# Two stacks of hybrid layers on one core: operands, sums of squares, factors and a bias table at the borders between projections

## The chip, the core and the metric

The kernel runs on one core of a Trainium2 chip. The metric is the device time of one execution in microseconds; less is better. The engines are named as in the profile: PE (TensorE), DVE (VectorE), ACT (ScalarE), POOL (GpSimd) and SP (SyncE, which here only issues DMAs).

## The reference

Two stacks of two layers each work on one sequence of 1024 positions by 1024 channels in float32. Cut to what matters for the change:

```python
# stack 1 (called stack 0 in the kernel), for both layers
h = rmsnorm(x, norm_g); proj = h @ w_in          # 28 blocks of 128 columns
y = concat(conv module, gated conv, windowed attention, neighbourhood attention with bias table)
x = x + y @ w_out                                # after both layers: x = rmsnorm(x, final_norm_g)
# stack 2 (stack 1 in the kernel), for both layers
u = rmsnorm(h, attn_norm); proj = u @ w_in       # 24 blocks
h = h + concat(retention, differential attention with ALiBi) @ w_out
h = h + (silu(u2 @ w_gate) * (u2 @ w_up)) @ w_down,   u2 = rmsnorm(h, ffn_norm)
out = rmsnorm(h, final_norm)
```

A row factor of an rmsnorm is 1/sqrt(mean of squares over the 1024 channels). Between the stacks two such norms follow each other directly.

## The kernel before

The activations lie transposed: `xt` holds 8 chunks of 128 channels by 1024 positions. A float32 product is made of three products of rounded parts: each operand is split into a high part and the rest. For the activations ACT rounds a chunk into `in_hi` (`split_hi`, line 1098) and DVE subtracts it into `in_lo` (`split_lo`, lines 1540 with gains and 1543 without); for the weights POOL does both (`split`, lines 597 and 601), one block of 128 output columns at a time, into two slots. SP loads the raw blocks (`load`, line 511). `product` (line 696) makes one output block: for each chunk three operand pairs, each with two matmuls of 512 columns, 24 steps with 8 chunks and 12 with 4. `between` is a list of other PE work that is put at evenly spaced steps inside the product. A product signals `done`; DVE takes its result out of PSUM with `evacuate` (line 1525, times the row factor `rfac`) or `add_to_x` (line 1531) and signals `taken`. Product n waits until block n - 2 is taken.

The row factor: ACT squares a chunk of x (`squares`, line 1102; `squares_of_half` also squares without the gain, line 1117, for the norm between the stacks), DVE adds the eight squares into one accumulator (`sum_squares`, line 1549; `sum_squares_x`, line 1575), PE sums over partitions (`row_sums`, line 716), DVE takes the inverse root and writes it on the diagonals of tiles (`row_factor`, lines 1597 to 1614), PE spreads it over all partitions (`spread`, line 724), ACT copies it to `rfac` (`take_factor`, line 1128). Before the change the squares lie in SBUF slots SQ and SQ_X.

The order of work is written out by hand for every engine, and each engine works through its own list in order, with semaphores between them. In stack 0 a layer has blocks 0 to 27 (projections, with attention, convolution and norms between them), 28 to 35 (first half of the output projection, chunks 0 to 3 of the mixed values) and 36 to 43 (second half). In stack 1 the blocks are 0 to 23, 24 to 31, 32 to 39 and 40 to 63 (FFN down projection). The last products of the second half are followed by the first product of the next layer, whose operands come from the x that they finish: `add_half` on DVE and `squares_of_half` on ACT work on that border.

The bias table of the neighbourhood attention is loaded by three DMAs from ACT's queue (line 1316), in pieces of 256 bytes, into `space_lo`, which is the memory of chunks 4 to 7 of `in_lo`; so ACT waits for the end of block 27 first. ACT then rounds chunks 1 to 3 for block 28, and takes the transposed values (`take_values`, line 1133).

## Time and profile before

| | us |
|---|---|
| median of 3 runs | 3616.26 |
| lowest and highest | 3616.20, 3618.64 |
| profiled execution, its own time | 3617.75 |
| its span in the profile | 3615.9 |
| PE busy | 3429.6 |
| POOL busy | 1353.8 |
| DVE busy | 1990.3 |
| ACT busy | 994.2 |

The profile is of one execution. A page has the busy time of each engine, the span in 40 slices, the chain of work that ended last, and groups of instructions by line. The trace behind it can be asked for the waits of an engine with what ended each, and for a timeline. In a timeline row the first number is the start and the second the time until the end; "x8" says that eight instructions are merged, and [7.14 <-DVE in_lo L1543] that the engine stood idle for 7.14 us until DVE's instruction of line 1543 let it go on.

### The profile page before, as it was taken

The numbers are of one execution on the slowest core, as the hardware profiler recorded it, in microseconds if no ns is written. First come the engines' busy times: TensorE is split into PE (matmuls) and PEld (weight loads), VectorE is DVE, ScalarE is ACT, GpSimd is POOL, SyncE is SP. The second block draws the span as 40 slices with busy tenths as digits, with TensorE's granted clock in tenths as the row PEclk, the third lists the DMA queues.
The fourth block names the chain that finished last, engine by engine and source line by source line (L and its number), as shares of the span: only waits on it lengthen the run. The fifth ranks groups of instructions, "written<-read, shape, count | busy, mean of one in ns | idle before, by whom it ended". The sixth has DMA issues, their size and how long they took to land.

```text
span 3615.9 us, 41963 instructions
## 1 busy us (share of the span) xinstructions
PE 3429.6 (95%) x16504; PEld 2769.6 (77%) x16504; DVE 1990.3 (55%) x2939; ACT 994.2 (27%) x1863; POOL 1353.8 (37%) x593
## 2 busy tenths in 40 slices
PE   7999899999898999898999999999998989999997
PEld 6877677877776888666888888888875778888886
DVE  5668536668547324577656642351438675565326
ACT  2220342130243000364333330010016543333101
POOL 3324213424303432203655534543220156554343
PEclk9999999999998999999999999999999999999998
DMA  4111203101201111102222252111110032223322
GB/s 147 42 31 52 55 13 87 42 30 53 67 7 35 41 50 38 53 1 93 72 86 88 82 198 81 52 53 54 35 64 7 16 125 77 86 88 120 131 87 76
DMA packets 72524, 236.31 MB, mean 65 GB/s; under 512 B 21920, under 2 KB 22304, under 8 KB 66208
## 3 DMA queue, kind: packets, MB, share of 16 engines
q1 hardware_dynamic: 50112, 205.54, 17.0%
q10 hardware_dynamic: 22240, 28.38, 2.7%
q8 instruction: 119, 1.95, 0.2%
q14 instruction: 53, 0.43, 0.0%
HBM read 193.00 MB, written 37.75 MB: 64 GB/s over the span
## 4 chain that ended last, share of the span: by engine, by line
PE 59%; DVE 6%; issue 1%; ACT 1%; DVEq 0%; ACTq 0%
PE ps L696 30%; PE ps L1063 23%; PE ps L759 2%; PE ps L823 1%; DVE space_hi L1660 1%; DVE xt L1531 1%; PE ps L806 0%; DVE st L1549 0%; DVE sl_r L2124 0%; ACT st L1166 0%; PE ps L983 0%; PE ps L979 0%; PE ps L735 0%; PE ps L834 0%; DVE small L1589 0%
## 5 line engine op out<-in xcount | busy, mean ns | idle before, releaser
L597 POOL TENSOR_TENSOR w_hi<-w_raw,ones_r 128x1024 fp32r<-128x1024 f32 x184 | 362.5, 1970 | 1836.6 <-PE ps L696 1813.7
L1063 PE MATMUL ps<-sl_r,sl_r 128*128 128x512 f32 x3696 | 843.9, 391 | 22.9 <-issue 22.9
L1063 PEld LDWEIGHTS ps<-sl_r,sl_r 128*128 128x128 f32 x3696 | 696.9, 189 | 168.8 <-issue 23.7
L696 PE MATMUL ps<-in_hi,w_hi 128*128 128x512 f32 x2176 | 700.4, 403 | 50.3 <-DVE in_lo L1540 19.5
L696 PE MATMUL ps<-in_hi,w_lo 128*128 128x512 f32 x2176 | 683.1, 395 | 0.0
L696 PE MATMUL ps<-in_lo,w_hi 128*128 128x512 f32 x2176 | 681.5, 395 | 0.0
L601 POOL TENSOR_TENSOR w_lo<-w_raw,w_hi 128x1024 fp32r<-128x1024 f32 x184 | 512.4, 2785 | 14.4
L696 PEld LDWEIGHTS ps<-in_hi,w_hi 128*128 128x128 f32 x2176 | 397.3, 190 | 156.8 <-issue 55.7
L696 PEld LDWEIGHTS ps<-in_lo,w_hi 128*128 128x128 f32 x2176 | 410.4, 190 | 91.2 <-issue 4.4
L696 PEld LDWEIGHTS ps<-in_hi,w_lo 128*128 128x128 f32 x2176 | 408.1, 190 | 92.2 <-issue 5.8
L696 PE MATMUL ps<-sl_r,w_hi 128*128 128x512 f32 x1408 | 378.5, 391 | 4.7 <-DVE sl_r L2166 4.7
L1525 DVE TENSOR_TENSOR st<-ps,rfac 128x1024 f32<-128x1024 f32 x104 | 127.2, 1223 | 410.2 <-PE ps L696 393.4
L641 POOL TENSOR_TENSOR sl_r<-sl,sl_r 128x1024 fp32r<-128x1024 f32 x88 | 212.5, 2416 | 343.9 <-ACT sl_r L1416 343.9
L1531 DVE TENSOR_TENSOR xt<-xt,ps 128x1024 f32<-128x1024 f32 x112 | 136.7, 1220 | 363.3 <-PE ps L696 362.3
L2134 DVE TENSOR_TENSOR sl_r<-raw_pair,sl_r 128x1024 fp32r<-128x1024 f32 x88 | 206.0, 2378 | 218.3 <-ACT sl_r L1416 218.2
L696 PEld LDWEIGHTS ps<-sl_r,w_hi 128*128 128x128 f32 x1408 | 265.5, 189 | 60.9 <-DVE sl_r L2166 5.6
L1180 ACT ACTIVATE st<-ps 128x384 f32<-128x384 f32 (+3 forms) x256 | 122.7, 479 | 348.9 <-PE ps L806 348.6
L696 PE MATMUL ps<-sl_r,w_lo 128*128 128x512 f32 x704 | 218.2, 391 | 0.0
L823 PEld LDWEIGHTS ps<-st 128*128 128x128 f32 x1504 | 184.4, 193 | 34.1 <-ACT st L1180 15.3
L823 PE MATMUL ps<-st 128*128 128x64 f32 (+1 forms) x1504 | 199.1, 275 | 5.8 <-DVE st L1709 5.8
L1808 DVE SCALAR_TENSOR_TENSOR st<-st,cur 128x1023 f32<-128x1023 f32 (+14 forms) x128 | 191.9, 1499 | 1.8
L1427 ACT ACTIVATE ps<-ps 128x512 f32<-128x512 f32 x132 | 76.8, 582 | 301.6 <-PE ps L1063 301.6
(198 smaller groups left out, 3457.1 us busy)
## 6 DMA issues: line engine op xcount, KB each, us to landing
w_raw<-w_in SPq DMA_DIRECT2D x184, 512.0 KB, 3.6
raw_pair<-w_ffn SPq DMA_DIRECT2D x44, 1024.0 KB, 4.9
hid_kept<-sl SPq DMA_DIRECT2D x44, 512.0 KB, 2.6
sl<-hid_kept SPq DMA_DIRECT2D x44, 512.0 KB, 7.3
x_put_away<-xt SPq DMA_DIRECT2D x16, 512.0 KB, 7.8
xt<-x_put_away SPq DMA_DIRECT2D x16, 512.0 KB, 6.4
xt<-x_in ACTq DMA_DIRECT2D x8, 512.0 KB, 9.1
space_lo<-c_alibi ACTq DMA_DIRECT2D x2, 2048.0 KB, 7.9
```

The source lines that it names most:

```text
L597: pool.tensor_tensor(w_hi[:, j, :], w_raw[:, j, :], ones[:, 0:1].broadcast_to([P, KC * P]), ALU.mult).then_inc(pool_own, 1)
L601: pool.tensor_tensor(w_lo[:, j, :], w_raw[:, j, :], w_hi[:, j, :].bitcast(F32), ALU.subtract).then_inc(w_split.handle, 1)
L641: pool.tensor_tensor(sl_r[:, RING[p % 2][lo], :], pair_sums(p)[i], sl_r[:, RING[p % 2][hi], :].bitcast(F32), ALU.subtract).then_inc(pair_s ...
L696: last = pe.matmul(ps[:, 2 * j + h, :], w[:, w_slot, (w_k + k) * P:(w_k + k + 1) * P], part[:, k0 + k, h * HALF:(h + 1) * HALF], start=(k ...
L823: last = pe.matmul(ps[:, 7, t * width:(t + 1) * width], turned_buffer(kind, g)[:, b * P:(b + 1) * P], value(t, kt), start=(kt == tiles[0]) ...
L1063: last = pe.matmul(ps[:, to[name], :], ring(sl_r, p, wp[w])[:, k * P:(k + 1) * P], half_of(sl_r, xp[x], k), start=(name in ("P1", "P5") an ...
L1180: act.activation(turned_buffer(kind, g)[:, 0:w], ps[:, 6, 0:w], ACT.Copy).then_inc(turned_out.handle, 1)
L1427: act.activation(to, ps[:, of, :], ACT.Copy).then_inc(carried.handle, 1)
L1525: dve.tensor_tensor(to, ps[:, 2 * j:2 * j + 2, :].rearrange("p a b -> p (a b)"), rfac[:, :], ALU.mult).then_inc(taken.handle, 1)
L1531: last = dve.tensor_tensor(xt[:, c, :], xt[:, c, :], flat(ps, 2 * (n % 2), 2), ALU.add)
L1808: return dve.scalar_tensor_tensor(acc[:, a:b], source[:, a + d:b + d], weight, acc[:, a:b], ALU.mult, ALU.add)
L2134: dve.tensor_tensor(lo, source, hi.bitcast(F32), ALU.subtract).then_inc(pair_lo.handle, 1)
```

## The change

- The squares of all borders but those at the FFN's entry go to PSUM banks 4 to 7, and DVE adds them from there. At the start of the kernel all chunks are rounded and subtracted first, and squared and summed behind that.
- Start: the second weight load waits for x chunk 3; DVE instead of POOL makes the first block's `w_lo`; three small DMAs are issued later; the lambda arithmetic of stack 1 moves behind evacuation 2. In layer 0 of stack 0 the row sums stand inside product 1; in both layers its spread moves from step 18 to step 21.
- Blocks 27 (stack 0) and 23 (stack 1): the product signals when chunks 0 to 3 have been read for the last time, and ACT and DVE write the operands of the next half from then on, DVE ahead of the block's evacuation. The last transposition of values moves from in front of block 28 (24) into block 29 (25). In stack 1 the ALiBi load and DVE's wait for it come later.
- The last product of stack 0's second half signals after each of its first three chunks, and chunks 4 to 6 are rounded then.
- Between the stacks nothing stands by itself any more: row sums, two spreads and the scaling of x by the first norm's factor lie inside products 0 to 2 and behind evacuations 1 to 3 of stack 1's layer 0.
- The bias table is laid out row by row in a DRAM tensor `bias_rows`, by three DMAs issued behind the first attention, and one DMA brings it to `space_lo` behind block 27.

The diff, cut to its core:

```diff
             def load(pair, first):
                 for j in range(2):
+                    if first and j:
+
+                        sp.wait_ge(x_in_sem[3].handle, 16)
                     if not first:
 
...
-            split(0, 0, 0)
+            pool.wait_ge(raw_in[0].handle, 16)
+            pool.tensor_tensor(w_hi[:, 0, :], w_raw[:, 0, :], ones[:, 0:1].broadcast_to([P, KC * P]),
+                               ALU.mult).then_inc(pool_own, 1)
+            pool.wait_ge(w_split.handle, 1)
+            pool.wait_ge(raw_in[1].handle, 16)
+            pool.tensor_tensor(w_hi[:, 1, :], w_raw[:, 1, :], ones[:, 0:1].broadcast_to([P, KC * P]),
+                               ALU.mult).then_inc(pool_own, 1)
+            pool.wait_ge(pool_own, 3)
+            pool.tensor_tensor(w_lo[:, 1, :], w_raw[:, 1, :], w_hi[:, 1, :].bitcast(F32),
+                               ALU.subtract).then_inc(w_split.handle, 1)
...
+                    if k in reads:
+                        last.then_inc(read.handle, 1)
...
-                pe.wait_ge(acc_ready.handle, acc_ready.at(0, l, 0))
-                row_sums(st[:, ACC, :])
-                block_of(1, between=[None, lambda: spread(diag_ready.at(0, l, 1))])
+                def sums():
+                    pe.wait_ge(acc_ready.handle, acc_ready.at(0, l, 0))
+                    row_sums(st[:, ACC, :])
+
+                if l:
+                    sums()
+                block_of(1, between=[None, None if l else sums, None, lambda: spread(diag_ready.at(0, l, 1))])
...
-                block_of(27, between=[None, lambda: evacuated(27), lambda: turn_values(0, l, 2, st[:, 8, :])])
-                evacuated(28)
-                turn_values(0, l, 4, st[:, 9, :])
+                block_of(27, between=[None, lambda: evacuated(27), lambda: turn_values(0, l, 2, st[:, 8, :])],
+                         read=first_read, reads=(3,))
+
+                def turn_last_values():
+                    evacuated(28)
+                    turn_values(0, l, 4, st[:, 9, :])
 
                 wait = chunk_wait(0, l, 0)
                 block_of(28, chunks=4, before_chunk=wait)
-                block_of(29, chunks=4)
+                block_of(29, chunks=4, between=[turn_last_values])
                 pe.wait_ge(vt_taken.handle, vt_taken.at(0, l, 6))
                 steps = attention(0, l, "na", ag["pieces"], ag["groups"], NB,
                                   lambda t, kt: st[:, 21 + kt // 4, (kt % 4) * 256 + t * HD:(kt % 4) * 256 + (t + 1) * HD],
...
+                    block_of(n, chunks=4, k0=4, read=tail_read, reads=range(3) if n == 43 else ())
...
+                def sums():
+                    if l == 0:
+
+                        pe.wait_ge(acc_x_ready.handle, DEPTH)
+                        row_sums(st[:, ACC_X, :], 7)
+                    pe.wait_ge(acc_ready.handle, acc_ready.at(1, l, 0))
+                    row_sums(st[:, ACC, :])
+
+                if l == 0:
+                    product(1, 0, 0, in_hi, in_lo, before_chunk=chunk_wait(1, 0, -8), between=[None, None, None, sums])
+                    product(1, 0, 1, in_hi, in_lo,
+                            between=[None, None, None, lambda: spread(diag_ready.mid(1), to=(4, 5))])
+                    product(1, 0, 2, in_hi, in_lo,
+                            between=[None, lambda: spread(diag_ready.at(1, 0, 1), DIAG_X, to=(6, 7))])
+                    product(1, 0, 3, in_hi, in_lo)
+                    products(1, 0, 4, 10)
+                else:
+                    product(1, l, 0, in_hi, in_lo, before_chunk=chunk_wait(1, l, -8))
+                    sums()
+                    product(1, l, 1, in_hi, in_lo, between=[None, lambda: spread(diag_ready.at(1, l, 1))])
+                    products(1, l, 2, 10)
 
...
+            def squares(c, scale=1.0, bank=None):
+
+                to = st[:, ACC, :] if c == 0 else flat(ps, bank, 2) if bank else st[:, SQ[c % 2], :]
+                act.activation(to, xt[:, c, :], ACT.Square, scale=scale).then_inc(squared.handle, 1)
...
+                        for k in range(3):
+                            act.wait_ge(tail_read.handle, tail_read.at(stack, l, k + 1))
+                            split([4 + k])
 
                     act.wait_ge(taken.handle, taken.at(stack, l, n + c + 1))
-                    if post:
-                        act.activation(st[:, ACC_X if c == 0 else SQ_X[c % 2], :], xt[:, c, :], ACT.Square
-                                       ).then_inc(squared_x.handle, 1)
-                    squares(c, post(c) if post else 1.0)
+                    act.activation(st[:, ACC_X, :] if c == 0 else flat(ps, 6, 2), xt[:, c, :], ACT.Square
+                                   ).then_inc(squared_x.handle, 1)
+                    squares(c, post(c), bank=4)
                     if c < 4:
                         split([c])
-                split(range(5, KC))
+                act.wait_ge(done.handle, done.at(stack, l, n + KC))
+                split([7])
 
             def take_factor(wait, slot=None, of=slice(5, 7)):
...
+            for c in range(KC):
                 if c >= 3:
 
                     act.wait_ge(dve_own, c - 2)
-                squares(c)
-
-            act.wait_ge(lam_exp.handle, 1)
...
                 act.dma_start(xt[:, KC - KEPT:KC, :], x_kept).then_inc(x_back.handle, 16)
+                raw = rpb_in[bass.ds(l, 1), :, :].rearrange("a g c -> (a g) c")[:, GRID_W - 1:GRID_W - 1 + GRID_W * (SKEW - 1)
+                                                                                ].rearrange("g (q s) -> q g s", s=SKEW - 1)
+                rows = bias_rows[l]
+
+                for to, of in ((rows[0:64], raw), (rows[64:128, 1:4 * ND], raw[:, 0:4 * ND - 1]),
...
+                act.wait_ge(first_read.handle, first_read.at(0, l, 1))
+                split_hi(0, lambda c: st[:, c, :], chunks=range(4))
                 act.wait_ge(done.handle, done.at(0, l, 28))
-                split_hi(0, lambda c: st[:, c, :], chunks=[0])
-                raw = rpb_in[bass.ds(l, 1), :, :].rearrange("a g c -> (a g) c")[:, GRID_W - 1:GRID_W - 1 + GRID_W * (SKEW - 1)
-                                                                                ].rearrange("g (q s) -> q g s", s=SKEW - 1)
-                table = flat(space_lo, 0, 4)[:, 0:4 * ND * GRID_W].rearrange("p (g c) -> p g c", c=GRID_W)
-
-                for to, of in ((table[0:64], raw), (table[64:128, 1:4 * ND], raw[:, 0:4 * ND - 1]),
-                               (table[64:128, 0:1], raw[:, 0:1])):
-                    act.dma_start(to, of[:, :, 0:GRID_W]).then_inc(bias_in.handle, 16)
-                split_hi(0, lambda c: st[:, c, :], chunks=range(1, 4))
+                act.wait_ge(rows_in.handle, rows_in.at(0, l, 48))
+                act.dma_start(flat(space_lo, 0, 4)[:, 0:4 * ND * GRID_W], bias_rows[l].rearrange("p g c -> p (g c)")
+                              ).then_inc(bias_in.handle, 16)
                 take_values(0, l, 4, lambda g: dv3(1, g))
 
                 act.wait_ge(lo_ready.handle, lo_ready.at(0, l, 1))
...
-            take_factor(spread_ready.mid(1), slot=FAC_X)
...
+                    take_factor(spread_ready.mid(1), of=slice(4, 6))
+                    take_factor(spread_ready.at(1, 0, 1), slot=FAC_X, of=slice(6, 8))
...
+                act.wait_ge(first_read.handle, first_read.at(1, l, 1))
+                split_hi(1, lambda c: st[:, c, :], chunks=range(4))
                 act.wait_ge(done.handle, done.at(1, l, 24))
                 act.dma_start(space_lo[:, :, :], c_alibi.rearrange("h p n -> p h n")).then_inc(alibi_in.handle, 16)
-
...
+                i = dve.tensor_tensor(st[:, ACC, :], st[:, ACC, :], flat(ps, bank, 2) if bank else st[:, SQ[c % 2], :], ALU.add)
...
+                    last = c == KC - 1
+                    if last:
+                        split([4])
                     add_to_x(stack, l, n + c, c)
                     if 1 <= c <= 4:
                         split([c - 1])
-                    if c == KC - 1:
-                        split([4])
+                    if last:
+                        split([5])
                     if c:
-                        if both:
-                            sum_squares_x(squared_x.at(stack, l, s0 + c + 1), c)
-                        sum_squares(squared.at(stack, l, s0 + c + 1), c)
-                split(range(5, KC))
+                        sum_squares_x(squared_x.at(stack, l, s0 + c + 1), c)
+                        if last:
+                            split([6])
+                        sum_squares(squared.at(stack, l, s0 + c + 1), c, bank=4)
+                split([7])
 
             def sum_squares_x(wait, c):
 
...
+                i = dve.tensor_tensor(st[:, ACC_X, :], st[:, ACC_X, :], flat(ps, 6, 2), ALU.add)
...
+            dve.wait_ge(pool_own, 2)
+            dve.tensor_tensor(w_lo[:, 0, :], w_raw[:, 0, :], w_hi[:, 0, :].bitcast(F32), ALU.subtract
+                              ).then_inc(w_split.handle, 1)
             for c in range(KC):
                 split_lo(0, 0, -8, lambda c: xt[:, c, :], lambda c: par[:, O_FIRST + c:O_FIRST + c + 1], chunks=[c])
-                if c:
-                    sum_squares(c + 1, c)
-            dve.wait_ge(const_in.handle, 16 * 2)
-            dve.wait_ge(lam_sem.handle, 16)
...
-                evacuate(0, l, 27, st[:, 9, :])
                 dve.wait_ge(conv_out.handle, conv_out.at(0, l, 2))
                 split_lo(0, l, 0, lambda c: st[:, c, :], chunks=range(4))
+                evacuate(0, l, 27, st[:, 9, :])
...
+                if l == 0:
+                    row_root(stat_ready.mid(1), D, bank=7)
+                    link(dve.tensor_copy(prior, root))
                 row_factor(stat_ready.at(1, l, 1), D, after=prior)
-                link(dve.memset(prior, 1.0))
-                dve.wait_ge(fac_ready.handle, fac_ready.at(1, l, 1))
+                if l == 0:
+                    diagonals(DIAG_X, 7)
+                    link(dve.memset(prior, 1.0))
...
+                    if l == 0 and k == 1:
+                        dve.wait_ge(fac_ready.handle, fac_ready.at(1, 0, 1))
+                    for c in ((), (0, 1), (2, 3, 4), (5, 6, 7))[k] if l == 0 else ():
+
+                        link(dve.scalar_tensor_tensor(xt[:, c, :], xt[:, c, :], par[:, O_FIN1 + c:O_FIN1 + c + 1],
+                                                      st[:, FAC_X, :], ALU.mult, ALU.mult))
...
-                evacuate(1, l, 23, st[:, 15, :])
 
                 dve.wait_ge(r_out.handle, r_out.at(1, l, NB))
                 split_lo(1, l, 0, lambda c: st[:, c, :], chunks=range(4))
+                evacuate(1, l, 23, st[:, 15, :])
+                add_to_x(1, l, 24, 0)
                 dve.wait_ge(alibi_in.handle, alibi_in.at(1, l, 16))
-                add_to_x(1, l, 24, 0)
                 add_to_x(1, l, 25, 1)
 
```

## Rows read from the trace of the kernel before

**Rows 1.** The page, busy time of each engine (share of the span) xinstructions.

```profile
PE 3429.6 (95%) x16504; PEld 2769.6 (77%) x16504; DVE 1990.3 (55%) x2939; ACT 994.2 (27%) x1863; POOL 1353.8 (37%) x593
```

**Rows 2.** Waits of PE: engine, line, releaser; us in total, times, longest.

```profile
PE ps L696 <- DVE in_lo L1543: 19.5, 8, 7.1
```

**Rows 3.** Timeline, inside a product: start us, us, engine, line, operation, count.

```profile
1144.07 0.61 PE L696 MATMUL ps<-in_hi,w_hi 128*128 128x512 f32 x2
1144.52 0.62 PE L696 MATMUL ps<-in_lo,w_hi 128*128 128x512 f32 x2
```

**Rows 4.** Timeline: a DVE sum alone, then two DVE operations beside POOL.

```profile
578.97 1.23 DVE L1575 TENSOR_TENSOR st<-st 128x1024 f32<-128x1024 f32 x1 [1.12 <-ACT st L1117]
...
585.45 2.63 POOL L597 TENSOR_TENSOR w_hi<-w_raw,ones_r 128x1024 fp32r<-128x1024 f32 x1 [9.94 <-PE ps L696]
...
586.36 1.22 DVE L1531 TENSOR_TENSOR xt<-xt,ps 128x1024 f32<-128x1024 f32 x1
...
588.15 3.27 POOL L601 TENSOR_TENSOR w_lo<-w_raw,w_hi 128x1024 fp32r<-128x1024 f32 x1
...
589.08 3.43 DVE L1575 TENSOR_TENSOR st<-st 128x1024 f32<-128x1024 f32 x1
```

**Rows 5.** Timeline of the start, first two products.

```profile
7.04 1.28 ACT L1229 ACT_TABLE_LOAD   x1 [7.04 <-issue]
...
9.61 6.18 DVE L1540 SCALAR_TENSOR_TENSOR in_lo<-xt,par,in_hi 128x1024 fp32r<-128x1024 f32 x2 [9.61 <-ACT in_hi L1098]
...
12.60 1.19 PE L696 MATMUL ps<-in_hi,w_hi 128*128 128x512 f32 x2 [12.60 <-DVE in_lo L1540]
...
32.07 1.84 PE L716 MATMUL ps<-ones_r,st 128*128 128x1 f32 x16
...
44.38 1.21 PE L724 MATMUL ps<-st_r,ones_r 128*128 128x512 f32 x4 [2.15 <-DVE st_r L1614]
...
46.75 1.23 DVE L1525 TENSOR_TENSOR st<-ps,rfac 128x1024 f32<-128x1024 f32 x1 [2.42 <-ACT rfac L1128]
```

**Rows 6.** View of the tensor x_in: its eight transfers, issued from 1.2 to 5.0.

```profile
DMA to landing us min/median/max: 6.5/9.1/13.0
```

**Rows 7.** Timeline of layer 0, stack 0, from the end of ACT's first attention.

```profile
350.60 2.19 ACT L1286 ACTIVATE st<-st 128x1024 f32<-128x1024 f32 x2 [80.43 <-DVE st L1906]
...
393.11 1.09 ACT L1133 ACTIVATE st<-ps 128x512 f32<-128x512 f32 x2 [9.69 <-PE ps L735]
...
395.38 9.58 ACTq L1316 DMA_DIRECT2D space_lo<-rpb_in  x3
...
407.38 1.22 PE L696 MATMUL ps<-in_hi,w_hi 128*128 128x512 f32 x2 [7.14 <-DVE in_lo L1543]
...
418.90 0.97 PE L777 MATMUL ps<-st_r 64*128 64x512 f32 x6
```

**Rows 8.** View of the tensor rpb_in: the six scattered table transfers of both layers.

```profile
DMA to landing us min/median/max: 7.4/9.2/12.6
```

**Rows 9.** Timeline, end of layer 0 of stack 0.

```profile
577.99 0.79 PE L696 MATMUL ps<-in_hi,w_hi 128*128 128x512 f32 x2 [2.68 <-DVE xt L1531]
...
580.28 1.05 PE L696 MATMUL ps<-in_hi,w_hi 128*128 128x512 f32 x2
...
594.89 0.73 PE L696 MATMUL ps<-in_hi,w_hi 128*128 128x512 f32 x2 [2.79 <-DVE in_lo L1540]
```

**Rows 10.** Timeline between the two stacks.

```profile
1157.59 3.57 PE L716 MATMUL ps<-ones_r,st 128*128 128x1 f32 x16 [10.64 <-DVE st L1575]
...
1162.18 0.17 DVE L1597 TENSOR_SCALAR ps<-ps 128x8 f32<-128x8 f32 x1
...
1167.66 2.08 PE L724 MATMUL ps<-st_r,ones_r 128*128 128x512 f32 x4 [6.50 <-DVE st_r L1614]
...
1170.90 10.53 DVE L1986 SCALAR_TENSOR_TENSOR xt<-xt,par,st 128x1024 f32<-128x1024 f32 x8 [3.21 <-issue]
```

**Rows 11.** Timeline of stack 1, layer 0, behind block 23.

```profile
1475.69 7.09 DVE L1543 TENSOR_TENSOR in_lo<-st,in_hi 128x1024 fp32r<-128x1024 f32 x4 [0.37 <-ACT in_hi L1098]
```

129 lines of the change are left out of this document (66 added, 63 removed).

## The prediction

> **What bounds the kernel now.** I read the page first. PE is busy for 3429.6 of the 3615.9 us [rows 1], so the change can take back only idle PE time, and time in which PE works at the lower clock after an idle stretch. Then the waits of PE, grouped by releaser: the largest group that the diff touches is products waiting for the low part of an operand, 19.5 us [rows 2]. Then the timeline around every longer wait. A product has 24 steps (8 chunks x 3 operand pairs), which stand 0.45 us apart [rows 3]: 10.9 us, or 5.44 us for a product of 4 chunks. What a border takes beyond that pace is its loss.
>
> Two things in the rows price everything below. **The lock:** a DVE operation whose two large inputs lie in SBUF takes 1.23 us alone, but started while POOL works it ends 1.1 us after POOL does: 3.43 us beside the POOL operation that ends at 591.42. With one input in PSUM it takes 1.22 us in the middle of a POOL operation [rows 4]. POOL splits a block of weights in two operations, right after a product ends, which is when DVE has most to do. **The clock:** behind a wait of 2.68 us PE goes on at 1.2 GHz for a while, steps 0.85 us apart instead of 0.45 [rows 9].
>
> The Trainium skill says the lock in its own way (page "SBUF — State Buffer", section "Who interferes with whom": a DVE instruction with two SBUF inputs is fully blocked by a GpSimd instruction that reads SBUF, one with at most one is not). By it the moved subtractions below stay exposed, which speaks against the edit at blocks 27 and 23; the rows price them so too.
>
> **The change part by part.**
>
> *Start (layer 0, stack 0).* Now: PE starts at 12.60, since the first two subtractions take 6.18 us beside POOL; row sums start at 32.07, the spread at 44.38 [rows 5]. After: the first ACT rounding needs no longer wait for three DMA issues (table load at about 5.5 instead of 7.04 [rows 5]), so it ends at 8.1; DVE computes w_lo of block 0 from 7.1 to 8.4 with POOL idle, subtracts chunk 0 by 9.7. PE starts at 9.75. The second weight block waits for x chunk 3 and lands near 15, so POOL's pair runs from 15 to 20 and delays two subtractions (about 3 us in all, as now). Eight subtractions of 1.28 us end near 22.3: the last x chunk lands at 18 (issued last, at 5.0, and the longest to land, 13.0 [rows 6]), rounded at 19, so DVE is last. Seven sums of 1.25 us follow instead of lying between: accumulator at 31.0. PE ends product 0 at 23.8, comes to the new place of the row sums (step 9 of product 1) at 27.9, waits 3.1, row sums to 32.8 (1.84 us); 5.5 us for roots and diagonals (1162.18 to 1167.66 [rows 10]) puts the spread at 38.4. That is 6.0 earlier than 44.38. If the 3.1 us wait brings the lower clock, the row sums take 3.57 as at 1157.59 [rows 10]: 4.3. I take **5.2** (3 to 7). The lambda arithmetic moved behind evacuation 2 (under 5 us of DVE) lies in the 11 us of product 3. The SP queue only loses its lead on block 1, which product 1 needs at 23.8.
>
> *Spread at step 21 instead of 18, layer 1.* Product 2 needs evacuation 0, which ends 3.6 us after the spread starts (44.38 to 47.98 [rows 5]). Behind step 21 PE has 3 steps and the spread, 2.4 us. Cost **1.2** (layer 0's is in the 3.6 kept above).
>
> *Blocks 27 to 29, twice.* Now: the three table DMAs hold ACT's issue for 9.58 us, so chunks 1 to 3 are rounded from 405.0 on, PE waits 7.14 us and starts slow; block 29 ends at 418.9 [rows 7]. After: ACT has the values at 394.2, rounds four chunks from there (1 us each). DVE subtracts from 395.3, POOL's pair starts at 395.4: whichever is first, the low parts come at about 396.6 to 398.5, 400 to 401.8, 402.9, 404.1. Block 28 ends at 405.7; evacuation 27 (405.4) is ahead of block 29, whose new inner part adds 0.9 to 1.1: 412.2. Gain 6.7, less about 0.9 because the waits that stay (4.8 us in all) may bring the lower clock: 5.8 each, **11.6** (8 to 13.5). Next late is DVE's first table half: query subtractions end at 411.2, so the table half ends at 413.4, as far behind block 29 as now. The three row copies now stand where ACT has 80.43 us with nothing to do [rows 7]: free; without that cover 9.6 us. The single load is issued at 398.2; even with the longest landing of the scattered form, 12.6 us [rows 8], it is there at 410.8, before DVE asks at 411.2.
>
> *End of layer 0 of stack 0.* Now 2.68 and 2.79 us of wait, each followed by five slow steps of 0.4 us extra [rows 9]: 9.2 us. Both come from SBUF sums held by POOL (3.43 and the like [rows 4]). After: both sums have an input in PSUM; a chunk costs DVE at most 1.22 + 1.28 + 2.44 = 5.0 us of the 5.44, with one subtraction open to the lock. Behind the last product: chunks 4 to 7 are subtracted at +0.7, +3.7, +6.9, +9.4 us after its end, and the next product asks for them at +5.4, +6.8, +8.2, +9.5. All covered, the last by a hair. Gain **9.2** (6 to 9.3). The ACT square written to PSUM has no row; its SBUF form takes 1.06, and I take the same (up to +0.2, off PE's path).
>
> *Between the stacks.* Now: 10.64 us wait, row sums at half clock (3.57 instead of 1.84), 6.50 us wait, spread slow (2.08 instead of 1.2), three slow steps (1.2) [rows 10]: 20.9 us. After: product 0 starts at once, operands as above; both row sums at its step 21, 3.4 us; two root chains (3.3 and 3.7 us) and the first diagonals (2.35) end near 1167.7, and PE is at step 21 of product 1 at 1170.8: no wait. Then 1.2 us for evacuation 0 as above. The eight scalings of x (1.3 us each [rows 10]) go between evacuations 1 to 3, of which PE asks one per 10.9 us. DVE first waits for the second factor until 1184.7 and has evacuation 2 done by 1192; PE asks for it at 1197. Gain 20.9 - 1.1 = **19.8** (16 to 20.5).
>
> *Stack 1, blocks 23 to 25, twice.* No table stood in ACT's way here. The four subtractions take 7.09 us under the lock and end at 1482.78 [rows 11]; started one POOL operation earlier they end at 1482.7 all the same, since POOL's pair still starts with the end of block 23. Evacuation 23 now follows them, and the value turn is moved into block 25, so its 1.1 us is no longer in a wait. Layer 0: -0.3; layer 1, where slow steps are in the time now, about +0.8 (an estimate); with the clock **-0.7** for both (-3 to +2). The later ALiBi load (1476.9) lands by 1485, before DVE asks.
>
> *FFN end and the rest:* no PE wait there now, nothing to gain; one PSUM buffer instead of two SBUF ones costs nothing because each square already waits for an addition queued behind the previous sum.
>
> **The sum:** 5.2 - 1.2 + 11.6 + 9.2 + 19.8 - 0.7 = 43.9 us. The profiled execution took 3617.75 (span 3615.9 and 1.85 around it), 1.5 above the median: 3617.75 - 43.9 = 3573.9, as a median 3572.4. I say **3572**.
>
> **Rivals.** *Waits shrink but stay* (0.20): the last subtraction has a cover of 0.1 us. If DVE is 2 to 3 us late there, at both ends of stack 0, each costs that and 1.9 us of lower clock, and the four places under the lock another 1 us each: 3572 + 9 to 13 = about **3583**. For: everything hangs on when POOL starts. Against: before the last chunk DVE has slack. *The edit doesn't do what it says* (0.06): the sums from PSUM are held by POOL too. Then 9.2 stays lost and the tail between the stacks is 5 us later: **3587**. Against: 1.22 us beside POOL [rows 4]. *Slower* (0.03): the copies of the bias rows go to DRAM in pieces of 256 bytes. ACT waits for them in front of the values of block 28, some 125 us behind their issue. Each us beyond 125 stops PE, twice; from 147 us on the kernel is slower than before (150 us: **3621**). Against: 12.6 us at most for the same pieces now [rows 8]. The Trainium skill bears on this (page "DMA: Bandwidth & Descriptors", "Specifications": below 512 B a transfer becomes read-modify-write); it names no factor, and no row here shows such a copy to DRAM. The forecast's own case, 3563 to 3579, has 0.70; 0.01 goes to no change.
>
> **How the numbers follow.** All best ends together give 3562, the first rival 3583, the second 3587, so 3562 to 3585 leaves out less than 2 in 10. About 0.2% (7 us) is what can be told from no change: faster 0.96, same 0.01, slower 0.03.
>
> **What would show it.** Right: PE starts near 9.8; the 7.14 wait is gone and waits of 1 to 3 us remain between the chunks of block 28; no PE wait over 1 us from the end of stack 0 to product 2 but the one for evacuation 0; DVE sums of 1.22 us beside POOL; stack 1's blocks 24 and 25 as long as before. Wrong: a wait at chunk 7 of the first product of a layer, steps 0.85 apart there, ACT idle in front of the bias load, or a wait of PE for row sums well over 3 us at the start.

## The result

The changed kernel takes 3570.7 us (median of 4 runs, 3570.65 to 3575.24) against 3616.2 us before (3614.28 to 3618.64): a ratio of 0.988, 95% interval 0.986 to 0.989. That is 45.5 us less, 1.3 under the forecast of 3572 and inside its range of 3562 to 3585. The profiled execution has a span of 3568.0 us, 47.9 less than the one of before; the ledger below adds up to these 47.9.

Two views of the page and the waits give the outline. First the busy line of the page:

```profile
PE 3417.0 (96%) x16504; PEld 2760.4 (77%) x16504; DVE 1960.6 (55%) x2939; ACT 993.6 (28%) x1863; POOL 1353.7 (38%) x592
```

Against [rows 1] PE has the same 16504 instructions and is busy 12.6 us less, and the mean granted clock of the execution is 0.988 against 0.982: work that ran at the lower clock (1.2 GHz) before runs at 2.4 GHz now. The other 35.3 us are idle time of PE that has gone. Then the waits of PE (engine, line, releaser: us in total, times, longest):

```profile
PE ps L715 <- DVE in_lo L1590: 16.2, 12, 1.7
PE ps L715 <- DVE st L1572: 11.2, 7, 2.4
...
PE ps L715 <- DVE in_lo L1587: 9.5, 1, 9.5
```

The group of [rows 2] (19.5 us in 8 waits, longest 7.1) is now 16.2 us in 12 waits, longest 1.7: the long waits went, and three short ones stand at each of four places (block 28 of both layers of stack 0 and block 24 of both layers of stack 1). The 9.5 of L1587 is the start of the kernel: PE's first matmul. The 11.2 of L1572 are waits for evacuations; one of them, 2.35 us in front of block 21, comes back below.

The ledger compares the end of each product block in the two traces (the events of the counter `done`); a gain is the change of the distance from one named block end to the next, and a minus sign is a loss.

| place | forecast us | measured us |
|---|---|---|
| start, to the end of block 2 | 5.2 | 8.6 |
| blocks 21 to 23, two layers | 0 | -1.8, -1.7 |
| blocks 28 and 29, two layers | 11.6 | 6.9 + 6.8 |
| block 30, two layers | 0 | -0.2, -0.2 |
| end of layer 0 of stack 0 | 9.2 | 4.55 + 4.55 = 9.1 |
| spread in layer 1 | -1.2 | -1.3 |
| between the stacks, to the end of block 2 | 19.8 | 19.8 + 0.8 - 2.35 = 18.3 |
| stack 1, blocks 24 and 25, two layers | -0.7 | -0.4, +1.4 |
| stack 1, attention, two layers | 0 | +0.6, +2.6 |
| small steps, rest | 0 | -0.8 |
| sum | 43.9 | 47.9 |

The ten lines miss by 16.8 us when every miss is counted, and by 4.0 in the sum.

**The start** (timeline: start us, us, engine, line, operation, count, idle before and its releaser):

```profile
8.10 8.45 DVE L1587 SCALAR_TENSOR_TENSOR in_lo<-xt,par,in_hi 128x1024 fp32r<-128x1024 f32 x7
9.52 1.19 PE L715 MATMUL ps<-in_hi,w_hi 128*128 128x512 f32 x2 [9.52 <-DVE in_lo L1587]
...
16.63 1.89 POOL L662 TENSOR_TENSOR w_hi<-w_raw,ones_r 128x1024 fp32r<-128x1024 f32 x1 [9.71 <-DMA w_raw<-w_in]
...
17.51 2.09 DVE L1587 SCALAR_TENSOR_TENSOR in_lo<-xt,par,in_hi 128x1024 fp32r<-128x1024 f32 x1 [0.97 <-ACT in_hi L1137]
...
19.52 8.73 DVE L1596 TENSOR_TENSOR st<-st,ps 128x1024 f32<-128x1024 f32 x7
...
28.31 1.95 PE L737 MATMUL ps<-ones_r,st 128*128 128x1 f32 x16 [0.79 <-DVE st L1596]
...
35.79 1.19 PE L745 MATMUL ps<-st_r,ones_r 128*128 128x512 f32 x4
```

PE starts at 9.52 instead of 12.60 [rows 5]. Seven subtractions take 8.45 us with POOL idle; POOL's pair starts only at 16.63, since weight block 1 has just landed, and only the eighth subtraction meets it (2.09). The seven sums from PSUM take 8.73 us although POOL splits weights beside most of them. The row sums start at 28.31, the spread at 35.79, against 32.07 and 44.38 [rows 5].

**Blocks 27 to 29** of layer 0, the answer to [rows 7]:

```profile
388.56 8.51 DVE L1590 TENSOR_TENSOR in_lo<-st,in_hi 128x1024 fp32r<-128x1024 f32 x4 [2.83 <-ACT in_hi L1137]
388.69 0.34 ACTq L1361 DMA_DIRECT2D space_lo<-bias_rows  x1
388.81 2.74 POOL L606 TENSOR_TENSOR w_hi<-w_raw,ones_r 128x1024 fp32r<-128x1024 f32 x1 [6.55 <-PE ps L715]
...
389.94 0.70 PE L715 MATMUL ps<-in_hi,w_hi 128*128 128x512 f32 x2 [1.28 <-DVE in_lo L1590]
391.62 3.24 POOL L610 TENSOR_TENSOR w_lo<-w_raw,w_hi 128x1024 fp32r<-128x1024 f32 x1
392.68 0.73 PE L715 MATMUL ps<-in_hi,w_hi 128*128 128x512 f32 x2 [1.12 <-DVE in_lo L1590]
...
396.00 0.74 PE L715 MATMUL ps<-in_hi,w_hi 128*128 128x512 f32 x2 [1.66 <-DVE in_lo L1590]
```

One issue of 0.34 us stands where three took 9.58; the wait of 7.14 is three waits of 1.28, 1.12 and 1.66, and none of them is followed by the lower clock. The four subtractions take 8.51 us beside POOL's two operations.

**The end of layer 0 of stack 0**, the answer to [rows 4] and [rows 9]:

```profile
570.01 3.28 POOL L610 TENSOR_TENSOR w_lo<-w_raw,w_hi 128x1024 fp32r<-128x1024 f32 x1
...
570.94 1.21 DVE L1626 TENSOR_TENSOR st<-st,ps 128x1024 f32<-128x1024 f32 x1
...
572.07 2.30 DVE L1587 SCALAR_TENSOR_TENSOR in_lo<-xt,cur,in_hi 128x1024 fp32r<-128x1024 f32 x1
...
575.43 1.27 DVE L1587 SCALAR_TENSOR_TENSOR in_lo<-xt,cur,in_hi 128x1024 fp32r<-128x1024 f32 x1
...
576.76 0.72 PE L715 MATMUL ps<-in_hi,w_hi 128*128 128x512 f32 x2
```

The sum with one input in PSUM takes 1.21 us inside a POOL operation; the subtraction with both large inputs in SBUF, right behind it, takes 2.30 and ends 1.08 after POOL does. The last low part ends at 576.70, 9.3 us behind the product that ended at 567.4, and PE's step that needs it starts at 576.76, only 0.06 us later. PE waits for none of them.

**Between the stacks**, the answer to [rows 10]:

```profile
1130.62 3.73 PE L737 MATMUL ps<-ones_r,st 128*128 128x1 f32 x32
...
1135.39 1.05 PE L715 MATMUL ps<-in_hi,w_lo 128*128 128x512 f32 x2
1136.25 1.05 PE L715 MATMUL ps<-in_hi,w_hi 128*128 128x512 f32 x2
```

Both waits of before are gone. But behind 32 matmuls of one column the steps stand 0.85 us apart for a while: PE was not idle, and the clock fell all the same.

How much of these 18.3 us each part brings is shown only for the sums: with them in SBUF 7.7 us are lost again (experiment 1), and in PSUM with the old order they bring 6.4, with two waits of 5.53 us left (experiment 5). The moving of row sums, spreads and scalings into the products was not run by itself.

### The profile page after: what moved, and what is told of

Read it like the earlier page. It is cut to its first block, busy times and chain, and to the rows that moved or that the text cites. A ratio compares the mean times of both kernels' runs of the same rounds, so it can differ in the third digit from the quotient of the medians.

```text
span 3568.0 us, 41967 instructions
## 1 busy us (share of the span) xinstructions
PE 3417.0 (96%) x16504; PEld 2760.4 (77%) x16504; DVE 1960.6 (55%) x2939; ACT 993.6 (28%) x1863; POOL 1353.7 (38%) x592
## 3 DMA queue, kind: packets, MB, share of 16 engines
q8 instruction: 119, 1.95, 0.2%
## 4 chain that ended last, share of the span: by engine, by line
PE 84%; DVE 11%; ACT 2%; issue 2%; DMA 0%; DVEq 0%; ACTq 0%
PE ps L715 48%; PE ps L1102 23%; PE ps L844 3%; DVE st L1876 3%; PE ps L827 2%; PE ps L780 2%; PE ps L798 2%; DVE space_hi L1720 1%; DVE in_lo L1590 1%; DVE st L1596 1%; DVE xt L1578 1%; PE ps L855 1%; ACT st L1221 1%; PE ps L737 1%; DVE sl_r L2194 0%
## 5 line engine op out<-in xcount | busy, mean ns | idle before, releaser
L1102 PEld LDWEIGHTS ps<-sl_r,sl_r 128*128 128x128 f32 x3696 | 696.8, 189 | 168.7 <-issue 23.7
L715 PE MATMUL ps<-in_hi,w_hi 128*128 128x512 f32 x2176 | 696.1, 401 | 37.8 <-DVE in_lo L1590 16.2
L1572 DVE TENSOR_TENSOR st<-ps,rfac 128x1024 f32<-128x1024 f32 x104 | 126.9, 1222 | 358.0 <-PE ps L715 341.0
```

The lines of the kernel that those rows point to most:

```text
L715: last = pe.matmul(ps[:, 2 * j + h, :], w[:, w_slot, (w_k + k) * P:(w_k + k + 1) * P], part[:, k0 + k, h * HALF:(h + 1) * HALF], start=(k ...
L1102: last = pe.matmul(ps[:, to[name], :], ring(sl_r, p, wp[w])[:, k * P:(k + 1) * P], half_of(sl_r, xp[x], k), start=(name in ("P1", "P5") an ...
L1572: dve.tensor_tensor(to, ps[:, 2 * j:2 * j + 2, :].rearrange("p a b -> p (a b)"), rfac[:, :], ALU.mult).then_inc(taken.handle, 1)
```

## The experiments

Each kernel is the changed one with the edit shown, except the fifth (the kernel before with an edit) and the tenth (the eighth with an edit). The edits are shortened; "..." and the comments stand for what was left out. Medians stand beside 3570.7 of the changed kernel, ratios against runs of the kernel before on the same chip. "Profile" is the change of the block ends in the profiled executions. Runs of one kernel spread over 2 to 7 us, and the kernel before has medians of 3616.0 to 3618.3 us on the chips used, so local readings rest on block ends, not on medians.

### 1. Sums in SBUF again

```
-  to = st[:, ACC, :] if c == 0 else flat(ps, bank, 2) if bank else st[:, SQ[c % 2], :]
+  to = st[:, ACC if c == 0 else SQ[c % 2], :]
   # and so for the squares of ACC_X and for both sums
```

> The changed kernel with every square written to SBUF again and every sum taken from SBUF; all orders stay new. My theory (the lock is what made the two waits at each end of stack 0, and early rounding alone can't remove them): a sum started beside POOL takes over 2 us again instead of 1.21, PE waits 1 to 3 us for the low parts of chunks 5 to 7 at the end of layer 0 of stack 0, with steps 0.85 us apart behind it, and the row sums of the start and between the stacks come later: 3570.7 + 6 to 15, about 3580. Rival (the early rounding with the counter inside the last product removed the waits; where the sums lie is of no account): 3570.7 + 2 at most.

Measured: 3594.4 us, ratio 0.994 (0.993 to 0.996): 23.7 us slower than the changed kernel. The mechanism of my theory, at one and a half times its upper size. By the profile the start loses 9.3, the end of layer 0 loses 4.55 + 2.56, the place between the stacks 7.3 + 0.4. Timeline of the start and of the end of layer 0:

```profile
19.87 14.63 DVE L1596 TENSOR_TENSOR st<-st 128x1024 f32<-128x1024 f32 x7
...
34.55 3.58 PE L737 MATMUL ps<-ones_r,st 128*128 128x1 f32 x16 [7.38 <-DVE st L1596]
```

```profile
568.05 3.26 POOL L610 TENSOR_TENSOR w_lo<-w_raw,w_hi 128x1024 fp32r<-128x1024 f32 x1
569.09 3.30 DVE L1596 TENSOR_TENSOR st<-st 128x1024 f32<-128x1024 f32 x1
...
573.79 0.98 PE L715 MATMUL ps<-in_hi,w_hi 128*128 128x512 f32 x2 [2.67 <-DVE xt L1578]
```

Seven sums take 14.63 instead of 8.73 us, PE waits 7.38 us for them and needs 3.58 for the row sums. What I had not priced: in the new order all seven sums of the start lie beside POOL's pairs, while in the old one most lay where POOL was idle. So the start's other edits (the new order, `w_lo` on DVE, the load held back, the row sums inside product 1) bring 10.0 - 9.3 = 0.7 us together at the end of block 1 when the sums stay in SBUF.

### 2. Old order of rounding, sums in PSUM

```
-  for k in range(3): act.wait_ge(tail_read.handle, ...); split([4 + k])
+  act.wait_ge(done.handle, done.at(stack, l, n + KC)); split([4])      # 5 to 7 behind the last square
   # DVE: chunk 4 behind the last addition to x, 5 to 7 behind the last sum
```

> The changed kernel with the old order of rounding and subtracting chunks 4 to 7 at the ends of stack 0 (chunk 4 rounded when the last product is done, 5 to 7 behind the last square; no counter inside the product); the sums stay in PSUM. My theory (PSUM sums carry the gain): by the durations of the trace of after (rounding 1.0, PSUM sum 1.21, subtraction 1.28) the low parts of chunks 5, 6 and 7 come 6.8, 8.1 and 9.4 us behind the last product, and are asked for at 6.8, 8.2 and 9.5: 3570.7 + 0 to 2. Rival (early rounding carries it): the two waits are back with their low clock, 4.6 us at the end of layer 0 and some of it between the stacks: 3570.7 + 5 to 10.

Measured: 3573.0 us, ratio 0.988 (0.987 to 0.990). In the profile no block end moves by over 0.3 us at either end of stack 0, and the span is 0.3 us shorter. The counter inside the last product and the new order of chunks 4 to 7 bring nothing that shows, once the sums are in PSUM. With the sums in SBUF (experiment 1 against before) they are worth 4.55 - 2.56 = 2.0 us at the first block of layer 1.

### 3. The table not laid out early

```
-  act.dma_start(rows[...], raw[...])  x3, behind the first attention; one load space_lo<-bias_rows here
+  act.dma_start(table[...], raw[...])  x3, here, behind the four roundings
```

> The changed kernel without the copies of the bias rows to DRAM: the three scattered loads go straight to the table's place, at the point behind the four roundings where the single load stands now. My theory (what held PE 7.14 us was that ACT issued the three loads between the rounding of chunks 0 and 1): the roundings stay where they are and PE's waits between chunks of block 28 stay 1.1 to 1.7 us; ACT issues until about 398.5, loads land by about 407, the values of block 28 are taken 0 to 4 us later than now: 3570.7 + 0 to 4. Rival (laying the table out early is what brings the gain): 6.9 us back in each layer: 3584.

Measured: 3573.8 us, ratio 0.989 (0.987 to 0.990). The profile shows no change at blocks 27 to 30 of either layer: DVE's first table half follows the query subtractions as before, with no wait for a load. The copy through DRAM and the early layout are worth nothing; what counts is that ACT issues behind the roundings. What differs is the start, +1.5 us, where nothing was edited (start of product 0's last slow step, row sums, the third step behind):

```profile
13.26 0.96 PE L715 MATMUL ps<-in_lo,w_hi 128*128 128x512 f32 x2
...
28.48 1.95 PE L737 MATMUL ps<-ones_r,st 128*128 128x1 f32 x16 [1.54 <-DVE st L1593]
...
31.52 1.06 PE L715 MATMUL ps<-in_hi,w_lo 128*128 128x512 f32 x2
```

Here the last slow step of product 0 starts at 13.26, in the changed kernel's profile at 14.78; so PE reached the row sums earlier, waited 1.54 instead of 0.79 us for the same DVE chain, and then the clock fell for a few steps. The start has one or the other of these two outcomes in every kernel below that keeps the new start with sums in PSUM.

### 4. POOL held until the four low parts are made

```
+  if low and j:      # only at blocks 27 and 23
+      pool.wait_ge(lo_ready.handle, lo_ready.at(stack, l, 4))
```

> The changed kernel with one wait more: at blocks 27 (stack 0) and 23 (stack 1) POOL splits the second half of its pair of weight blocks only when the low parts of the four chunks are made. My theory (PE's waits of 1.12 and 1.66 us in front of chunks 2 and 3 there are the lock: DVE subtractions of 2.3 us and more beside POOL): they go, and what is left is the 1.28 us in front of chunk 0: 2.8 us less at each of four places, 3570.7 - 11 = 3559.5. Rival (DVE's chain behind, the query subtractions and the first half of the table, is as late as the block, or the weights POOL now splits later come too late): 3 us of gain at most.

Measured: 3561.0 us, ratio 0.985 (0.983 to 0.987): 9.7 us better than the changed kernel.

```profile
389.87 4.63 DVE L1592 TENSOR_TENSOR in_lo<-st,in_hi 128x1024 fp32r<-128x1024 f32 x4 [2.83 <-ACT in_hi L1139]
...
391.24 0.71 PE L717 MATMUL ps<-in_hi,w_hi 128*128 128x512 f32 x2 [1.28 <-DVE in_lo L1592]
...
394.67 1.90 POOL L608 TENSOR_TENSOR w_hi<-w_raw,ones_r 128x1024 fp32r<-128x1024 f32 x1 [11.11 <-DVE in_lo L1592]
```

Four subtractions take 4.63 instead of 8.51 us, only the 1.28 in front of chunk 0 is left, and block 28 is 3.39 us shorter in both layers, block 24 of stack 1 too: 13.5 us in the profile. Of these, 1.4 go back at the start (its other outcome) and 3.0 in the attention of stack 1, layer 1. There the granted clock differs over the same block, first the changed kernel, then this one (window, us, PE busy, granted clock, DMA share, GB/s):

```profile
2653.90:2719.40 65.50, 59.55 (x305) 0.97 0.06 17
```

```profile
2642.10:2709.00 66.90, 60.89 (x305) 0.95 0.05 17
```

### 5. The kernel before, with its sums in PSUM and nothing else

```
   # before.py: squares of the start and of the ends of stack 0 to PSUM, summed from there
+  pe.wait_ge(acc_ready.handle, acc_ready.at(1, 0, 0))      # in front of row_sums(ACC_X)
```

> The kernel before with one part of the change: squares of the start and of the ends of stack 0 go to PSUM and are summed from there; all orders stay as before (sums between the subtractions, old rounding, row sums of both accumulators in front of the first product of stack 1, which now wait for both). My theory, from the first two experiments: the 9.1 us at the end of layer 0 are all there (block 43 and block 0 4.5 us each shorter); at the start the sums interleaved with the subtractions lose nothing once POOL is done, so little is gained there (0 to 3); between the stacks the chain sums, roots, spread stays in front of the product: 3616 - 10 to 15, about 3604. Rival (the parts need each other; the old orders keep the waits): 3 us at most at the end of layer 0, about 3612.

Measured: 3602.9 us, ratio 0.996 (0.995 to 0.998): 13.1 us faster than before. The end of layer 0 gains 4.55 + 4.51, all that the whole change gains there, and 6.4 come between the stacks. At the start it loses 1.4 (a clock drop behind a wait); why it gains nothing there is seen in product 0:

```profile
20.45 1.21 DVE L1550 TENSOR_TENSOR st<-st,ps 128x1024 f32<-128x1024 f32 x1
20.59 0.73 PE L696 MATMUL ps<-in_hi,w_hi 128*128 128x512 f32 x2 [0.79 <-DVE in_lo L1541]
```

With sums between the subtractions DVE needs 2.45 us for a chunk (a sum each 2.45 us, this one at 20.45) and PE 1.36, so PE waits about 0.8 at every chunk, as in the kernel before. At the start neither part works alone: the other edits 0.7, the place of the sums -1.4, all together 10.0 at the end of block 1. In this profile blocks 21 to 23 lose 1.8 us in either layer, and stack 1 gains about 4, with no edit at either place.

### 6. Without SP's wait for x chunk 3

```
-  if first and j: sp.wait_ge(x_in_sem[3].handle, 16)
```

> The changed kernel without SP's wait for x chunk 3 ahead of weight block 1. My theory (the wait keeps POOL's first pair away from the first subtractions): POOL splits block 1 from about 7 or 8 us on, DVE's w_lo and subtractions 0 to 3 stand under the lock, PE starts at 10.5 to 12.5 instead of 9.5; but the last subtraction is then alone (1.3 instead of 2.1 us), and the sums end 0.8 us earlier if the last x chunk lands as before. As the sums end the start, the whole is within 1.5 us of 3570.7. Rival (the wait is what gave the gain above the forecast at the start, 3 us): 3574.

Measured: 3574.7 us (3571.7 to 3578.5), ratio 0.988 (0.987 to 0.990).

```profile
8.46 1.89 POOL L659 TENSOR_TENSOR w_hi<-w_raw,ones_r 128x1024 fp32r<-128x1024 f32 x1 [1.34 <-DVE w_lo L1802]
...
9.00 12.93 DVE L1584 SCALAR_TENSOR_TENSOR in_lo<-xt,par,in_hi 128x1024 fp32r<-128x1024 f32 x8 [0.61 <-ACT in_hi L1134]
...
11.58 1.19 PE L712 MATMUL ps<-in_hi,w_hi 128*128 128x512 f32 x2 [11.58 <-DVE in_lo L1584]
```

PE starts at 11.58, as my theory has it. But the last chunks of x also land later (the last rounding starts at 18.15 instead of 16.33), so the sums end 2.3 us later and not earlier, and block 1 ends 3.7 later. That is what the wait is worth at the start, my rival's price; part of it is the start's other outcome. The step of my theory that failed is "if the last x chunk lands as before". The profile is of the slowest of the four runs; 3.1 of the 7.2 us that it is longer come in the attention of stack 1, layer 1.

### 7. Without the counter at blocks 27 and 23

```
-  act.wait_ge(first_read.handle, ...); split_hi(0, ..., chunks=range(4)); act.wait_ge(done.handle, done.at(0, l, 28))
+  act.wait_ge(done.handle, done.at(0, l, 28)); split_hi(0, ..., chunks=range(4))      # so also in stack 1
```

> The changed kernel with the first four chunks rounded only when block 27 (stack 0) or 23 (stack 1) is done, as before, not when its fourth chunk has been read; the table stays early. My theory (the three table issues in the middle of the roundings made the 7.14 us wait; the counter brings only ACT's head start of 1.3 us, and that shortens PE's first wait): block 28 becomes 1.0 to 1.5 us longer in each of four places: 3570.7 + 4 to 6. Rival (the counter is what brings the 6.9 us): 3570.7 + 12 or more.

Measured: 3579.5 us, ratio 0.990 (0.988 to 0.991): 8.8 us slower than the changed kernel, between my theory (4 to 6) and the rival (12 or more). Block 28 is longer by 0.5 in layer 0 and 1.95 in layer 1, block 24 of stack 1 by 1.7 and 2.4. The first row is layer 0, the second layer 1:

```profile
391.96 0.70 PE L715 MATMUL ps<-in_hi,w_hi 128*128 128x512 f32 x2 [3.27 <-DVE in_lo L1588]
```

```profile
944.66 1.19 PE L715 MATMUL ps<-in_hi,w_hi 128*128 128x512 f32 x2 [3.62 <-DVE in_lo L1588]
```

A wait of 3.27 us is followed by the full clock, one of 3.62 by the lower one. Later rounding makes the first wait 2 us longer and costs only 0.5, since POOL's pair then meets fewer subtractions, but the longer wait brings the clock down at three of four places. So the counter is worth 0.5 by itself and about 2 where it keeps the clock up, 6.5 in all; the rest of the 10.2 us that the profile adds is clock elsewhere (1.6 us between the stacks, and stack 1's attention). Of the 6.9 us at block 28 it brings 0.5 to 2.

### 8. Four placements more

The hold of the fourth experiment stays in, and these are added:

```
+  pool.wait_ge(lo_ready.handle, lo_ready.at(0, 0, 0))       # POOL's pair of the start, behind the last subtraction
   # the turn of values of blocks 27 and 23 in the second quarter of the product, not its last third
   # layer 1: spread at step 18;  between the stacks: row sums of ACC_X at step 15, of ACC at step 21
```

> The changed kernel with POOL held as in the fourth experiment and four placements more: the turn of values inside blocks 27 and 23 moved from their step 20 to step 12, so that ACT can round before the product ends; the spread of layer 1 of stack 0 at step 18 again; the row sums of the two accumulators between the stacks apart, at steps 15 and 21; POOL's pair of the start held until the last subtraction. My theory: the 1.28 us in front of chunk 0 goes at four places (5.1), the spread gives back 1.3, the row sums 0.9 if 32 one-column matmuls in a row were what brought the lower clock there, the start 0.8: 3561.0 - 5 to 8, about 3554. Rival (the work behind is late anyway: the second turn, the attention's first scores): 3561 - 2 at most.

Measured: 3551.5 us (3551.3 to 3553.8), ratio 0.982 (0.981 to 0.983): 64.5 us faster than before and 19.2 faster than the changed kernel. (The turn stands at step 9, not 12 as the text on record has it.) By the block ends against experiment 4: the spread gives 1.4, block 24 of stack 1 1.5 in each layer, block 28 of stack 0 only 0.3, the row sums 1.7; the start's 1.2 is its better outcome. POOL's hold at the start gives nothing: the last subtraction takes 1.28 instead of 2.09, but the sums then wait 0.57 us for ACT's squares. Between the stacks:

```profile
1119.19 1.84 PE L740 MATMUL ps<-ones_r,st 128*128 128x1 f32 x16
...
1123.75 1.84 PE L740 MATMUL ps<-ones_r,st 128*128 128x1 f32 x16
```

The granted clock over block 1 of stack 1, first the changed kernel, then this one:

```profile
1136.50:1149.30 12.80, 12.77 (x52) 0.92 0.14 42
```

```profile
1127.10:1138.90 11.80, 11.80 (x52) 1.00 0.17 45
```

The same 32 small matmuls in two groups of 16, six steps apart, and the clock stays up. In all eight traces that have the 32 in a row (the changed kernel, experiments 1 to 4, 6, 7 and 9) the granted clock fell during or right behind them; in the two that have them apart (experiments 8 and 10) it did not.

### 9. The three loads back between the roundings

```
   split_hi(0, ..., chunks=[0]); act.wait_ge(done.handle, done.at(0, l, 28))
+  act.dma_start(table[...], raw[...])  x3
   split_hi(0, ..., chunks=range(1, 4))
```

> The changed kernel with the three scattered loads of the bias table back between the rounding of chunk 0 and that of chunks 1 to 3 in stack 0; the early rounding of chunk 0 by the counter stays, and so does the rest. My theory (their place in ACT's program is what cost 7.14 us, not their form or their time of landing): ACT issues from 388.7 to 398.3, chunk 1 is rounded at 399.3, PE waits about 6 to 8 us in front of chunk 1 and goes on at the lower clock: block 28 becomes 6 to 9 us longer in each layer, 3570.7 + 12 to 18. Rival (with chunk 0 early the rest hides behind it): 3570.7 + 6 at most.

Measured: 3588.9 us, ratio 0.992 (0.991 to 0.994): 18.2 us slower than the changed kernel, 15.9 in the profiles; the kernel before is 2.0 slower on that chip too. It is my theory, at the upper end of its 12 to 18.

```profile
390.27 9.33 ACTq L1359 DMA_DIRECT2D space_lo<-rpb_in  x3
...
399.65 2.95 ACT L1137 ACTIVATE in_hi<-st 128x1024 fp32r<-128x1024 f32 x3 [9.61 <-issue]
...
402.02 1.22 PE L715 MATMUL ps<-in_hi,w_hi 128*128 128x512 f32 x2 [8.88 <-DVE in_lo L1588]
```

Block 28 is 8.0 and 7.8 us longer in the two layers. ACT's issue of 9.33 us stands in front of the rounding, and PE waits 8.88 behind it at the lower clock. With experiment 3 this closes the case: the same three loads cost 8 us in front of chunk 1 and nothing behind chunk 3.

### 10. The eighth kernel without POOL's hold

```
-  run(stack, l, first, half_end, 2, low=True)
+  run(stack, l, first, half_end, 2)
```

> The eighth experiment's kernel without POOL's wait for the four low parts at blocks 27 and 23; all four placements stay. My theory (the lock only counts where DVE's subtractions and POOL's pair fall together): in stack 1 the early turn lets all four low parts end before block 23 does, so POOL's pair meets none of them and block 24 stays as short as in the eighth experiment; in stack 0 the first rounding stands at 387.1 behind the convolution's output, DVE's subtractions meet POOL's pair and block 28 becomes 1.5 to 3 us longer in each layer: 3551.5 + 3 to 6. Rival (the hold carries all of the gain at the four places): 3551.5 + 11.

Measured: 3558.5 us, ratio 0.984 (0.982 to 0.985); 3.7 us longer than the eighth in the profile; its median is 7.0 higher, of which 2 are the kernel before on that chip (3618.3 against 3616.0). Stack 0 first, then stack 1:

```profile
387.99 8.51 DVE L1596 TENSOR_TENSOR in_lo<-st,in_hi 128x1024 fp32r<-128x1024 f32 x4 [2.56 <-ACT in_hi L1143]
```

```profile
1420.19 4.63 DVE L1596 TENSOR_TENSOR in_lo<-st,in_hi 128x1024 fp32r<-128x1024 f32 x4 [7.25 <-ACT in_hi L1143]
```

In stack 1 the turn of values came early enough for all four subtractions to end about when block 23 does (at 1424.8; the block ends at 1424.4), so POOL slows none and the hold is not needed. In stack 0 the rounding stands behind the convolution's output (DVE is at it until 385.7), meets POOL's pair, and block 28 is 3.4 us longer in each layer. My size for this, 1.5 to 3, was a little low.

## Why the prediction was right, and where it was not

The time and the mechanism came out; the sum is right to 4 us in 48 only because errors of 16.8 us in all stand on both sides, which is in part luck.

**Start (5.2, measured 8.6).** The mis-sized terms are the two landings. "The second weight block ... lands near 15, so POOL's pair runs from 15 to 20 and delays two subtractions": it started at 16.63 and delayed one, by 0.8. "The last x chunk lands at 18": it was rounded from 16.33. So the subtractions ended at 19.6 instead of 22.3, and the 3.1 us wait for the row sums was 0.79. PE's start (9.75, measured 9.52) and the sums (7 of 1.25, measured 8.73 in all) were right. The earlier end of the subtractions brings the spread 2.6 us earlier than forecast, which with the 6.0 of the case without a clock drop makes the 8.6. That the clock might fall there was right as a risk: in experiments 3, 4 and 9 it does, and then the gain is 6.9 to 7.2.

**Blocks 27 to 29 (11.6, measured 13.7).** Block 28 was to end 10.35 us behind block 27 and did so after 10.38. The waits sum to 4.1, not 4.8, and the allowance of 0.9 for the lower clock was not needed; the forecast before that allowance was 6.7, measured 6.9. But the forecast took the early layout of the table and the place of the issues in ACT's program as one; experiments 3 and 9 put the gain on the place and nothing on the layout, and experiment 7 gives 0.5 to 2 us of it to the counter.

**End of layer 0 (9.2, measured 9.1).** Low parts at +0.7, +3.7, +6.9 and +9.4 us behind the product were forecast; the trace has +0.8, +3.6, +7.0 and +9.3, and the last is asked for 0.06 us after it is there. A cover that thin, 0.1 us forecast, was luck as much as reckoning. The cause I gave, the sums in PSUM, is shown by experiments 1, 2 and 5: they alone bring it all, and the early rounding beside them nothing.

**Between the stacks (19.8, measured 18.3).** The failed step is "both row sums at its step 21, 3.4 us": they took 3.73, and the clock fell behind them, of which nothing was in the sum. Experiment 8 gets back 1.7.

**Spread (-1.2, measured -1.3)**: right, and given back by experiment 8.

**Stack 1, blocks 24 and 25 (-0.7, measured +1.0).** In layer 0 -0.4 against -0.3 forecast, in layer 1 +1.4 against an estimate of 0.8.

**Not in the sum at all:** blocks 21 to 23 (-3.5) and the attention of stack 1 (+3.2). Neither has an edit. In front of block 21 PE waits 2.35 us for an evacuation in both kernels, 2.32 in layer 1 of the changed one. The clock over that block, first before, then after (both layer 0), then experiment 1 in layer 1, where the wait is 2.34:

```profile
307.70:321.30 13.60, 11.16 (x48) 1.00 0.14 39
```

```profile
299.20:314.40 15.20, 12.85 (x50) 0.89 0.11 34
```

```profile
867.70:882.60 14.90, 12.56 (x55) 1.00 0.12 36
```

With the clock at 0.89 block 21 is 1.6 us longer. That moves POOL's split to where DVE's convolution works (three operations of it take 7.41 us, before 6.44), and so blocks 22 and 23 shift too. In experiments 1, 7, 9 and 10 layer 1 gets about 1.7 of this back, with nothing edited there. "Nothing to gain" in the rest was wrong as a claim that nothing would move: each shift of the work above deals these drops anew, by 1 to 3 us a place. I did not find what decides which of two equal waits is followed by the lower clock. The Trainium skill says of it (page "TensorE: Matmul & The Clock Gate", section "Part 1: The HAM clock gate") that the same kernel can show a different number of slow matmuls from run to run, at its start. The runs agree in so far as three of the changed kernel's four took 3570.7 us at a mean granted clock of 0.988 and the fourth 3575.24 at 0.987; the two outcomes of the start stand in traces of different kernels, and no kernel here has two traces.

**The rivals.** *Waits shrink but stay* did not come: no wait for a low part at either end of stack 0. *PSUM sums held by POOL* is refuted by 1.21 us inside a POOL operation of 3.28, beside 3.30 for the SBUF form in experiment 1. *Slower through the bias copies*: the six of them landed 6.0 to 10.9 us after their issue, not later than the scattered loads [rows 8]. The rule of the Trainium skill on the shared port (page "SBUF — State Buffer", section "Who interferes with whom") spoke against the moved subtractions; it held, 8.51 us for four against 4.63 with POOL held, and it cost what the forecast had put in. I had not drawn the other conclusion from it, that POOL can be held for the 6 us without loss.

**Sums to put right.** Three side sums of the forecast come out otherwise when they are added again: all best ends together give about 3565, not 3562; the second rival 3586, not 3587; the slower case at 150 us 3622, not 3621. The forecast of 3572 does not rest on them.

## What to carry to other kernels

Where two engines lock each other, look at both: put one input of a DVE operation in PSUM where that can be done, and hold the other engine where it can't; here the second was one wait and worth as much (9.7 us) as the first at the end of layer 0 (9.1). An engine's DMA issues count as work in its program: the same loads cost 8 us in front of a rounding that PE waits for, and nothing behind it. Parts of a change can be worth nothing alone and 10 us together, so a sum part by part needs the time of the engine that sets the pace with and without each of the others.

## What the runs showed of the hardware

- The granted clock fell behind 32 one-column matmuls in a row (3.73 us) with PE never idle in the changed kernel, and in all eight traces that have them in a row; two groups of 16 of 1.84 us did not bring it down (two traces).
- Waits of 1.54, 2.35 and 3.62 us were followed by the lower clock, others of 2.35 and 3.27 were not: the length of a wait alone does not decide.
- Four subtractions with both large inputs in SBUF take 8.51 us beside two POOL operations and 4.63 alone; a sum with one input in PSUM takes 1.21 us inside a POOL operation.
- Copies into DRAM in pieces of 256 bytes landed in 6.0 to 10.9 us, the same pieces into SBUF in 7.2 to 12.3.
